# A feed-forward's down product by seven block products, its operand sums made in other stages

## What is computed

```python
D_MODEL, SEQ, D_FF, FFN_CONV = 1024, 1024, 2816, 3

def conv_glu_ffn(h, w_up, conv_w, conv_b, w_down):
    u = causal_dwconv(h @ w_up, conv_w) + conv_b
    a, b = jnp.split(u, 2, axis=-1)
    return (jax.nn.silu(a) * b) @ w_down

h = x
y = hybrid_mixer(rmsnorm(h, g[0]), ...)
h = h + rmsnorm(y, g[1])
y = memory_cross_attention(rmsnorm(h, g[2]), rmsnorm(mem, mem_norm_g[l]), ...)
h = h + rmsnorm(y, g[3])
y = conv_glu_ffn(rmsnorm(h, g[4]), ffn_w_up[l], ffn_conv_w[l], ffn_conv_b[l], ffn_w_down[l])
h = h + rmsnorm(y, g[5])
```

## Time and profile before

| | us |
|---|---|
| median of 3 runs | 2691.1 (2685.81 to 2692.93) |
| the profiled execution | 2688.15 |
| its span in the trace | 2686.4 |
| TensorE busy | 2593.3 (97%) |
| VectorE busy | 1665.2 (62%) |
| GpSimd busy | 1132.5 (42%) |
| ScalarE busy | 843.6 (31%) |
| TensorE's share of the chain that ended last | 88% |

### The profile page before, as it was taken

One profiled execution on the slowest core, in us unless ns is written; L12 is line 12 of the kernel. 1 busy time (PEld: TensorE's weight loads), 2 busy tenths in 40 slices (PEclk: granted clock), 3 DMA queues, 4 the chain that ended last, 5 costly groups with the idle time before them and its releaser, 6 DMA issues.

```text
span 2686.4 us, 33150 instructions
## 1 busy us (share of the span) xinstructions
PE 2593.3 (97%) x13218; PEld 2175.0 (81%) x13218; DVE 1665.2 (62%) x2192; ACT 843.6 (31%) x1332; POOL 1132.5 (42%) x651
## 2 busy tenths in 40 slices
PE   6999989989999999999999999999999999999998
PEld 5788778877788877888888887888888888888887
DVE  4879967767513488666673467815455465476566
ACT  4011223324323333333332436312222222243342
POOL 2433100036641638877764443764222322242364
PEclk9999999999999999999999999999999999999999
DMA  4122333235311412222245453573433442475682
GB/s 152 56 93 96 98 122 127 83 99 205 126 63 63 157 65 79 87 79 87 79 138 197 163 185 118 188 258 118 134 102 110 133 138 97 153 262 207 224 313 110
DMA packets 147381, 360.25 MB, mean 134 GB/s; under 512 B 15173, under 2 KB 51229, under 8 KB 147100
## 3 DMA queue, kind: packets, MB, share of 16 engines
q1 hardware_dynamic: 65072, 177.81, 19.8%
q10 hardware_dynamic: 82156, 180.33, 18.9%
HBM read 268.90 MB, written 89.19 MB: 133 GB/s over the span
## 4 chain that ended last, share of the span: by engine, by line
PE 88%; DVE 6%; ACT 2%; POOL 2%; issue 1%; DMA 1%; ACTq 0%; DVEq 0%; POOLq 0%
PE pp L296 31%; PE pp L2178 13%; PE pp L494 11%; PE pp L278 9%; PE pp L2231 8%; PE pp L2918 2%; PE pp L1255 2%; POOL w_lo L3617 1%; PE pp L1942 1%; PE pp L1921 1%; POOL w_hi L3615 1%; PE pp L1534 1%; PE pp L444 1%; PE pp L2939 1%; PE pp L2938 1%
## 5 line engine op out<-in xcount | busy, mean ns | idle before, releaser
L3615 POOL CAST w_hi<-w_raw 128x1024 fp32r<-128x1024 f32 x184 | 220.5, 1198 | 996.0 <-PE pp L296 671.0
L296 PE MATMUL pp<-w_hi,act_hi 128*128 128x512 f32 x1344 | 536.7, 399 | 14.8 <-POOL w_lo L3617 9.4
L296 PE MATMUL pp<-w_lo,act_hi 128*128 128x512 f32 x1344 | 525.0, 391 | 0.0
L296 PE MATMUL pp<-w_hi,act_lo 128*128 128x512 f32 x1344 | 524.7, 390 | 0.0
L3617 POOL TENSOR_TENSOR w_lo<-w_raw,w_hi 128x1024 fp32r<-128x1024 f32 x184 | 469.8, 2553 | 14.7
L296 PEld LDWEIGHTS pp<-w_hi,act_hi 128*128 128x128 f32 x1344 | 253.3, 188 | 70.4 <-POOL w_lo L3617 10.2
L296 PEld LDWEIGHTS pp<-w_hi,act_lo 128*128 128x128 f32 x1344 | 252.9, 188 | 53.7
L296 PEld LDWEIGHTS pp<-w_lo,act_hi 128*128 128x128 f32 x1344 | 253.6, 189 | 48.4
L2149 POOL TENSOR_TENSOR w_lo<-w_raw,w_hi 128x1024 fp32r<-128x1024 f32 x52 | 133.8, 2574 | 164.1 <-ACT w_hi L2143 163.9
L494 PE MATMUL pp<-act_hi,w_hi 128*128 128x512 f32 x480 | 191.3, 399 | 11.1 <-DVE act_lo L835 6.5
L494 PE MATMUL pp<-act_lo,w_hi 128*128 128x512 f32 x480 | 189.6, 395 | 0.0
(11 more groups left out here) (467 smaller groups left out, 5292.1 us busy)
## 6 DMA issues: line engine op xcount, KB each, us to landing
w_raw<-in_weights SPq DMA_DIRECT2D x314, 512.0 KB, 3.5
z_s<-hg_st ACTq DMA_DIRECT2D x52, 512.0 KB, 3.9
hid_s<-ffn_cb ACTq DMA_DIRECT2D x22, 512.0 KB, 2.6
ffn_graw<-hid_s ACTq DMA_DIRECT2D x44, 256.0 KB, 3.2
hg_qkb<-hT_s SPq DMA_DIRECT2D x16, 512.0 KB, 8.2
qkvT_s<-mixin_o ACTq DMA_DIRECT2D x12, 512.0 KB, 2.8
gdn_qkv<-qkvT_s ACTq DMA_DIRECT2D x8, 768.0 KB, 6.1
front_x<-in_x ACTq DMA_DIRECT2D x8, 512.0 KB, 5.2
```

Of the source, the lines that this page charges most:

```text
L296: last = pe.matmul(dst, a[:, k, t * P:(t + 1) * P], columns(w, j, k, 0, n), start=(k == 0 and a is high and w is w_hi), stop=(k == NK - 1 ...
L3615: pool.tensor_copy(hi, raw).then_inc(w_split, 1)
```

## The change

The down product becomes seven block products as well. The gated channels form 2 x 2 blocks: the token half (first or second index of the block: which half of 512) and whether the channel tile is even or odd; the weights form 2 x 2 blocks by channel tile and by half of the columns. `DOWN` lists the seven pairs: hidden block or sum (A11, A12, A22, S1 to S4), weight block or sum (B11 to B22, T1 to T4). Each pair is 11 steps (`FG`) of 4 token tiles x 3 matmuls, 77 steps and 924 matmuls in all where there were 44 steps and 1056. Two steps share a weight half; the sixth half of each pair holds only 512 columns.

- *Weight sums.* `DownSums` loads the down weights, 11 blocks of 1 MB, makes T1, T3, T2, T4 in place (four subtractions of 128x512) and stores 11 x 1 MB in a scratch tensor. VectorE makes six of them in Queries, GpSimd five in Attention, ahead of its split of the second output strip. ScalarE issues every load and store, between its copies. Its stores' landing is waited for at the start of `xo`.
- *Sums of gated channels.* After every second `gated`, VectorE makes S1, S3, S2, S4 (four of 128x512) and ScalarE stores them; the eleventh group is made at steps 6 and 8 of the down product.
- *Pieces.* Six buffers for `graw` and five each for `gh` and `gl`, in place of four.
- *Results.* Products 0 and 1 add up in banks 0 to 3, 2 to 4 in banks 4 to 7, 5 and 6 in banks 0 to 3. ScalarE copies two of the results (`keep`), VectorE adds the others out of PSUM (`join` u, v, e, f, g: 4 each of 128x512).
- *Norm.* The norms of tiles 0 to 3 now stand at steps 56 to 76 of 77 (`FIRSTS`, `SECONDS`, `HIGHS`, `TURNS`).
- *Hand-over.* HgInputs waits for the last join before its second product rather than after it.

```diff
-FCHUNKS = ((0, 1, 2, 3), (4, 5, 6, 7))
+DOWN = (("A11", "B11"), ("A12", "B21"), ("S2", "T2"), ("S1", "T1"), ("S4", "B22"), ("S3", "T3"), ("A22", "T4"))
+DOWN_HALVES = (FG + 1) // 2
+N_DOWN = len(DOWN) * DOWN_HALVES // 2
...
+        class DownSums:
+            BY_DVE = 6
...
+            def make(self, eng, S, k, n):
+                b11, b12, b21, b22 = (self.bufs[k % 3][:, i, :] for i in range(4))
+                eng.wait_ge(self.loaded[k % 3], self.loaded_before + 16 * (k // 3 + 1))
+                S.done(eng.tensor_tensor(b11, b12, b11, ALU.subtract), "T1")
+                S.done(eng.tensor_tensor(b12, b22, b12, ALU.subtract), "T3")
+                after(eng, S, "T3", n)
+                S.done(eng.tensor_tensor(b22, b22, b11, ALU.subtract), "T2")
+                after(eng, S, "T2", n)
+                S.done(eng.tensor_tensor(b21, b21, b22, ALU.subtract), "T4")
...
+            def finish(self, act):
+                self.store(act, FG - 1)
+                self.landed(act)
+
+            LOADS = {4: (0,), 5: (1,), 6: (2,), 10: (3,), 11: (4,), 12: (5,)}
+            STORES = {7: 0, 8: 1, 9: 2, 13: 3, 14: 4, 15: 5}
+            LATE_LOADS = {0: (6, 7), 1: (8,), 5: (9,), 6: (10,)}
+            LATE_STORES = {3: 6, 4: 7, 5: 8, 7: 9}
...
# Attention.act, behind the copy "hi" of tile t
+                    if t in W.LATE_STORES:
+                        W.store(act, W.LATE_STORES[t])
+                    for k in W.LATE_LOADS.get(t, ()):
+                        W.load(act, k)
...
# Ffn.pe
-                    for a, b in ((0, 0), (0, 1), (1, 0)):
-                        for h in range(2):
-                            last = pe.matmul(pp[u][:, h * 512:(h + 1) * 512], g[a][:, u * P:(u + 1) * P], w[b][:, h * 512:(h + 1) * 512],
...
+                    for a, b in ((0, 0), (0, 1), (1, 0)):
+                        last = pe.matmul(self.down_bank(p, u), g[a][:, u * P:(u + 1) * P], w[b], start=(fresh and k == 0 and a == 0 and b == 0),
+                                         stop=(k == FG - 1 and a == 1), skip_group_check=True)
...
+            TURNS = {68: 0, 71: 1, 74: 2}
+            FIRSTS = {56: 0, 59: 1, 63: 2, 67: 3}
+            SECONDS = {63: 0, 67: 1, 70: 2, 73: 3}
+            HIGHS = {69: 0, 72: 1, 75: 2}
...
# Ffn.act, down product
+                for n in range(self.STEPS):
+                    p, k = n // FG, n % FG
                     high(n + 2)
-                    cast_down(n + 3)
-                    load(n + 4)
+                    if k % 2 == 0:
+                        cast_down(p * DOWN_HALVES + k // 2 + 3)
+                    load(n + 6)
...
# Ffn.dve, up product
+                    if r % 2 == 0:
+                        hidden_sums(r // 2 - 1, "S1", "S2")
...
# Ffn.dve, down product
+                joins = {2: "u", 3: "v", 4: "e", 5: "f"}
+                for n in range(self.STEPS):
+                    p, k = n // FG, n % FG
+                    if n + 2 < self.STEPS:
                         low(n + 2)
                     if n == 1:
                         conv(FT - 1, "b")
+                    elif n == 4:
                         gated(FT - 1)
+                    elif n == 6:
+                        hidden_sums(FG - 1, "S1")
+                    elif n == 8:
+                        hidden_sums(FG - 1, "S2")
...
+                    if k == FG - 1 and p in joins:
+                        join(p, joins[p])
+                    if n in self.SECONDS:
+                        N_.normalise(dve, self.SECONDS[n])
+                    if n in self.FIRSTS:
+                        N_.scale(dve, self.FIRSTS[n])
+                    if n in self.HIGHS:
+                        N_.low(dve, self.HIGHS[n])
+                join(len(DOWN) - 1, "g")
+                N_.low(dve, 3)
                 N_.scale(dve, 4)
-                for t in range(1, NT // 2):
-                    N_.low(dve, t)
```

More of the change, by code:

```diff
@@ L563, in act @@
                 R, HT = self.norm, self.HT
+                if self.sums:
+                    self.sums.finish(act)
                 R.load_gains(act)
@@ L631, in __init__ @@
                 self.qT = self.buf("qT", [P, NK, T])
+                self.sums = DownSums(prev.source)
             def pe(self, pe):
@@ L661, in act, with dve @@
                 R.settled(act)
+                W = self.sums
                 for j in range(NT // 2, 2 * NK):
                     keep(j)
+                    if j in W.STORES:
+                        W.store(act, W.STORES[j])
+                    if j == NT // 2 + 2:
+                        after(act, R.N, "xn", NT - 1)
+                    for k in W.LOADS.get(j, ()):
+                        W.load(act, k)
+            def dve(self, dve):
+                self.sums.dve(dve)
         def taps(dve, V, name, rnd, dst, src, w, n, bias=None, amid=None):
@@ L2353, in act, with first @@
                         self.cast(act, i + 1, "A12", "A22")
+                        if r % 2 == 0:
+                            store_sums(r // 2 - 1)
                     else:
                         cast_down(2)
[L2356 to L2361 removed]
+                def first(t):
+                    after(act, self.joined, f"e{t}" if t < NT // 2 else f"g{t - NT // 2}", 0)
+                    N_.first(act, t)
@@ L2379, in first @@
-                def first(t):
-                    after(act, self.kept, "kept", t)
-                    N_.first(act, t)
-                self.keep(act, 4)
+                    elif n == 21:
+                        keep(1, "c")
+                    if n in self.SECONDS:
+                        N_.second(act, self.SECONDS[n])
+                    if n in self.FIRSTS:
+                        first(self.FIRSTS[n])
+                    if n in self.HIGHS:
+                        N_.high(act, self.HIGHS[n])
@@ L2397, in act @@
                 first(7)
-            def keep(self, act, t):
-                c = [t in tiles for tiles in FCHUNKS].index(True)
-                after(act, self.down_made, "made", t)
-                self.kept.done(act.activation(self.y[:, t, :], pp[t - FCHUNKS[c][0]][:, :], ACT.Copy), "kept")
             def dve(self, dve):
@@ L3607, in _ @@
                 for i in range(HALVES[j]):
+                    if j == FIRST_STRIP["o"] + 1 and i == 0:
+                        xq.sums.pool(pool)
                     r, q = RAW_AT[j] + i, PART_AT[j] + i
@@ L3731, in weight_stream @@
         out += [*wide(w["w_out_2"][0], 0, N_OUT)]
-    assert len(out) == NHALVES
+    assert len(out) == NHALVES - 2 * N_DOWN
     return np.stack(out)
```

295 lines of the change are left out of this document (202 added, 93 removed).

## The result

Predicted was 2687 us (2671 to 2702), within 0.3% of before at 0.40, faster at 0.38. Measured, on one chip by turns: 2693.5 us (median of 20 runs, 2685.9 to 2700.5) against 2687.3 for the kernel before (20 runs), a ratio of 1.0021 with a 95% interval of 1.0012 to 1.0030. A second set gave 1.0017 (1.0006 to 1.0029). So the change costs some 5 us where a gain of 3 was forecast: within 0.3%, but surely not faster. The forecast time was counted from 2691.1, the median of three runs of the kernel before; twenty have 2687.3, from which the same sum gives 2684. The profiled execution has a span of 2690.3, against 2686.4.

The account below looks back on a forecast made before the run. TensorE, busy 97% of the span, was taken as the bound. Terms of -29.9, +2.5, +10.3, +2.7, +2, +0.5, +8 and +0.5 gave -3.4 us; against the median of 2691.1 that is 2687.7, stated as 2687 (2671 to 2702).

Parts of the forecast that it names:

- the prediction's own signs of being wrong: Down product not shorter by 13 to 19 us, or TensorE waiting in the queries or for w_raw.
- Removed work, -29.9: Down product: 924 matmuls for 1056, 132 fewer at 0.2267 us each, all on the path: -29.9 us.
- Start, +2.5: Start of the down product: remainders behind convolutions on VectorE come late for TensorE's shorter steps: +2.5 us (1.5 to 3.5).
- The four early norms, +10.3: Late down product: normalise, scale and collisions delay remainders, so TensorE waits at steps 66, 70, 73: +10.3 us (6 to 14).
- The first rival (no squeeze): Collisions fall between and five pieces' lead absorbs the norms: their term 2, hand-over 0, total -14.4, 2677 us; chance 0.15.
- Transfers, +0.5: Down product: more pieces and the gains with mod at step 20 delay weight loads, TensorE hardly: +0.5 us (0 to 4).
- Hand-over, +2.7: After the down product: VectorE's joins, scales and normalises put transpose 7 at 30.7 us, not 27.9: +2.7 us (0 to 6).
- Attention, +8: Attention: VectorE's four scalings collide with GpSimd's weight sums, once less the spare time, once in full: +8 us (2 to 13).
- The second rival (it doesn't pay): Attention's scalings don't collide, or sums and scalings miss each other: total -11.4, 2680 us; chance 0.22.
- Up product, +2: Up product: hidden sums on VectorE delay combination c21 by 0 to 0.5 us in each of ten groups: +2 us (0 to 5).
- the third rival (every group late): Up product: one more GpSimd instruction of 1.28 us ahead of a sum in each of ten groups: +9.4, 2700 us; chance 0.21.
- Queries, +0.5: Queries' stage: VectorE's weight sums fit in free time, ScalarE's loads and stores too; +0.5 us (0 to 3) for the barrier.

Follow-up runs that it names:

- Experiments 3 and 4: Changed kernel with early norms at other steps: 1.0012 of the kernel before; with each norm's VectorE half two or three steps behind ScalarE's second pass: 0.9992.
- Experiment 1: Changed kernel with z's slots in the order 4, 5, 2, 3, 0, 1: 1.0002 of the kernel before; the kernel before with that order: 1.0015.
- experiment 6: Changed kernel with z's slots reordered, GpSimd's sums gated behind scalings, norm halves apart and mod's load cut in three: 2677.9 us, 0.9965 of the kernel before.
- the last kernel: experiment 6 plus last early transpose sooner, last channel's convolutions later, bounds' four instructions behind the up product's third channel: 2672.9 us, 0.9943 of the kernel before.
- experiment 5: Changed kernel with mod's 1.5 MB load cut in three at steps 28, 35 and 41, VectorE waiting at step 50: 1.0003 of the kernel before.

## Why the prediction was wrong

The step that failed first of all is the price of a wait: every wait was entered at its own length and the lower clock behind it at nothing, and that clock measured 6.5 us in all. The reuse of the slots by z was entered at nothing, and measured 3.9. "TensorE not at all" for the transfers, entered at 0.5, measured 3.3, and the hand-over was taken at half its size. Two terms on the other side were too high, the norms by 2.3 and the attention by 5.6 (8 where 2.4 were waited); it is luck that these took 7.9 off a miss of 15. Two of the prediction's own signs of being wrong came: the down product is shorter by 12.4 and not by 13 to 19, and TensorE stands behind a late `w_raw`.

The parts miss by +4.2 (down product), +3.8 (hand-over), +3.9 (z), -3.7 (attention), -0.5 (queries) and +0.2 (up product); the rest is chance (-0.6). That makes the 7.3 between -3.4 and +3.9.

- **Removed work, -29.9: right.** 924 matmuls, 0.2267 apart where nothing waits.
- **Start, +2.5: right** (2.5).
- **The four early norms, +10.3: right in mechanism and place, 2.3 too high.** The waits are 6.3, 0.6 and 2.7, together 9.6, where the walk had 6.3, 2.4 and 3.1, together 11.9; from both go the 1.6 of before. Experiments 3 and 4 bear out both halves of it, VectorE's load and its standing still. The first rival (no squeeze) fell.
- **Transfers, +0.5: failed**: "TensorE not at all" was read from a stage whose steps were twice as long. The late weight was seen; what hangs on it at half the step was not walked. It measured 3.3, and 4.9 with the clock. Transfers +2.8, clock +3.6, norms -2.3 make the down product's miss of 4.2 up to 0.1.
- **Left out, the clock**: +3.6 inside the down product (1.7 and 2.0 behind two waits), 1.0 of the hand-over's, behind tile 7, and 1.9 of the attention's: 6.5. The kernel before shows a granted clock of 0.80 and 0.77 in the windows after its own wait there, 1662 to 1670; I didn't look, and took a wait to cost its length.
- **Hand-over, +2.7: right in kind, half its size.** VectorE sets the pace there as forecast, but the walk took tile 4's scale to be as before, ahead of the end. It now stands behind the joins: 5.4.
- **Left out, the slots of z**, +3.9. The change turned an even number of strips odd; what reuses their slots, 180 us later, was not looked at. Experiment 1 shows it both ways.
- **Attention, +8: mis-sized**, +4.3. L2068 (L1987 of before) does collide. The first meeting put four scalings back by 3.2 and not 4.6, and TensorE by 2.4; the other 1.9 are the clock. The meeting with the last sums, counted in full, didn't come: they start 1.5 us behind the scalings. The second rival (it doesn't pay) fell.
- **Up product, +2: right in sum, wrong in shape.** Not ten groups of 0.2, but one of 1.7 to 2.0 at the first; the third rival (every group late) fell.
- **Queries, +0.5**: nothing (66.50 before and after).

Waits of 2 to 3.5 us were not always followed by the lower clock: behind a wait of 2.9 in experiment 1 only 0.1 us were lost, behind 3.5 in the last kernel 0.1; behind 1.9 in experiment 6 it came, and behind the same 2.7 at the output product's start it came in the kernel before and not in the changed one. What decides that is open. Open too is what makes the closing stage vary by up to 6 us from execution to execution; no edit went with it.

## What to carry to other kernels

Halving the step of the bounding engine halves the cover of everything else: walk again each stall that the old step hid, those that belong to no edited line too. Count what an edit does to the parity of a shared ring, and look where the ring is used next. And test parts of 2 to 5 us by the start times of a stage's first matmuls and by its single waits, in more than one execution, not by medians of runs that spread over 10.

## What was not expected of the hardware

A wait of TensorE can cost more than its length, as the windows show. The Trainium skill (TensorE: Matmul & The Clock Gate, "What's actually happening") says that the half rate is the idle state and that work releases it. After 3.3 us of waiting the granted clock was 0.63 over the next 4 us, after 6.3 us it was 0.51, and the stretch at the lower level, some eight matmuls, added 1.7 to 2.0 us. Without the wait (experiment 5) the clock was 1.00 and the 1.7 were gone. So mending a wait of 3.3 gave back 4.9.
